# Inverting the delta rule's chunk matrices with one product and its transpose per level, in four quarters of the array

## The chip, the cores and the metric

The kernel runs on one NeuronCore of a Trainium2 chip. TensorE (PE in the profile) multiplies, VectorE (DVE), ScalarE (ACT) and GpSimd (POOL) do the elementwise work, SyncE (SP) issues the loads. The metric is device time in microseconds (us) of one launch; less is better. A difference is a change if it exceeds what repeated runs of one kernel differ by.

## The reference

A 512-token sequence of width 1024 goes through two blocks in float32: a hybrid mixer (gated delta rule with 4 heads of 128, beside a convolution of 31 taps), cross attention over a memory, a convolved feed-forward, then a retention layer and a stick-breaking attention layer. The part that matters here is the chunked delta rule, 8 chunks of 64 tokens for each of 4 heads:

```
kb = kc * bc[..., None]
L = jnp.where(strict, jnp.einsum('nbhid,nbhjd->nbhij', kb, kc) * decay, 0.0)
rhs = jnp.concatenate([vc * bc[..., None], kb * jnp.exp(gc)[..., None]], axis=-1)
sol = lax.linalg.triangular_solve(eye + L, rhs, left_side=True, lower=True, unit_diagonal=True)
```

So 32 unit lower triangular 64x64 matrices `I + L` have to be inverted (or solved with). The kernel forms the inverses on TensorE by doubling: blocks of 1, 2, 4, ..., 32 are joined until the 64x64 block is inverted.

## The kernel before

Large projections fill most of the program. A weight slab of 128x1024 is loaded, rounded to its high part by ACT (L1307) and its low part by DVE (L2054), and then multiplied with the activations in three matmuls of 512 columns for each of 8 steps of the contraction (L507 to L509): 24 large matmuls to a slab. Small work is laid between them by "beats": after the third, sixth and eighth step of a slab (so after 9, 9 and 6 large matmuls) each of three lanes of generator functions goes on to its next `yield`. All engines tick the same lanes in the same places, each in its own program order, and wait for each other by semaphores.

The delta rule is a lane function `chain(p)`, one for each pair of heads p = 0, 1; each handles 16 matrices (2 heads x 8 chunks). Even chunks lie on partitions 0 to 63 and odd ones on 64 to 127 (`RR`), so a 64x64 product has its operands and its result in one half: product after product alternates between the upper left and the lower right quarter of the array. `chain(0)` starts with the slab of the first GLU, `chain(1)` 27 beats later. The order in a chain is: Gram matrices (`kk`), transposes of v, `qk`, then the inverse, then keys, `u`, `w`, eight state steps of two beats each (`ws`, then `kv` and `o`), and a transpose of the output (`otr`): 37 ticks. From the first tick of `chain(1)` to the end of the keys-and-gates section there are 3 + 12 + 20 = 35 beats; whatever is left then runs without large matmuls between it (`fg.drain()`).

The inverse keeps the current block inverse both ways round: `UTT` (transposed) and `UT`. At each of the levels 2, 4, 8, 16, 32 POOL masks `UL` to the block that joins (`LM`, L3070), TensorE multiplies it with `UT` (`lt`, 16 products), DVE forms I minus that (`UX`, L2188), and at the next beat TensorE makes the new transposed inverse (`tt`, 16 products) and the new plain one (`tx`, 16 products, left out at the last level). DVE copies the one out of PSUM (L2198; at the last level in two halves into `UTF`, L2203), ACT the other (L1439). The first level, blocks of 1, is done elementwise on DVE (L2178, L2181), and its transpose `tl` is 16 products with the identity. So a level takes two beats. The products of pair 0 use tiles `km`, `u_xq` and `u_x`, those of pair 1 `u_t`, `u_rq` and `u_r`; all are issued by the helper `one` at L512. The results go to banks 4 and 5 (pair 0) or 2 and 3 (pair 1). DVE also works on the convolutions meanwhile: four taps for each conv tile (L2106 to L2114) and the 31 taps of two of the four long convolutions (L2266, L2271), the other two going through ACT (L1505) and POOL (L3090).

Of the kernel before, what the change touches and what calls it, by code (L numbers as in the profile page):

```python
# [1 line left out]

# [31 lines left out]
CSH = ["id64", "mc", "ms", "m1t", "m2t", "m4t", "m8t", "m16t", "m32t"]  # L34
# [132 lines left out]
def program(nc, A, out):  # L167
    root = ExitStack()
    with root:
# [11 lines left out]
        PS = [root.enter_context(nc.psum_tensor(f"ps{i}", [128, 512], F32)) for i in range(8)]  # L181
# [165 lines left out]
        LM = [[R3[p][:, i * 512:i * 512 + 512] for i in range(2)] for p in range(2)]  # L347
        KBANK = ((4, 5), (2, 3))
        WQ = [x[:].rearrange("p (g y c) -> p g y c", y=4, c=64) for x in (XWQ, UWQ)]
# [12 lines left out]
        LEVELS = (2, 4, 8, 16, 32)  # L362
# [130 lines left out]
        def tensor_program(e):  # L493
# [17 lines left out]
            def one(dst, a, b, start, stop):  # L511
                return e.matmul(dst, a, b, start=start, stop=stop, skip_group_check=True)  # L512
# [178 lines left out]
            def chain(p):  # L691
# [31 lines left out]
                pe.wait_ge(*gdv[(p, "tt", 0)])  # L723
                for h, tb, par in CHUNKS:
                    o = (h * 4 + tb) * 64
                    R = RR[par]
                    t = one(b[R, o:o + 64], UTT[p][R, o:o + 64], csh["id64"][R, :], True, True)
                t.then_inc(*gmm((p, "tl")))
                rel[A_] = [(gac, (p, "tl", 0))]
                yield  # L730
                for n_ in range(5):
                    b = bank(A_)
                    pe.wait_ge(*gac[(p, "tl", n_)])
                    pe.wait_ge(*ggp[(p, "lm", n_)])
                    for h, tb, par in CHUNKS:
                        o = (h * 4 + tb) * 64
                        R = RR[par]
                        t = one(b[R, o:o + 64], LM[p][n_ % 2][R, o:o + 64], UT[p][R, o:o + 64], True, True)
                    t.then_inc(*gmm((p, "lt", n_)))
                    rel[A_] = [(gdv, (p, "xx", n_))]  # L740
                    yield
                    b = bank(B_)
                    pe.wait_ge(*gdv[(p, "xx", n_)])
                    pe.wait_ge(*gdv[(p, "tt", n_)])
                    for h, tb, par in CHUNKS:
                        o = (h * 4 + tb) * 64
                        R = RR[par]
                        t = one(b[R, o:o + 64], UX[p][R, o:o + 64], UTT[p][R, o:o + 64], True, True)
                    t.then_inc(*gmm((p, "tt", n_)))
                    rel[B_] = [(gdv, (p, "tt", n_ + 1))]  # L750
                    if n_ < 4:
                        b = bank(A_)
                        for h, tb, par in CHUNKS:
                            o = (h * 4 + tb) * 64
                            R = RR[par]
                            t = one(b[R, o:o + 64], UTT[p][R, o:o + 64], UX[p][R, o:o + 64], True, True)
                        t.then_inc(*gmm((p, "tx", n_)))
                        rel[A_] = [(gac, (p, "tl", n_ + 1))]
                    yield
# [8 lines left out]
                for h in range(2):  # L768
                    b = bank(KBANK[p][h])
                    pe.wait_ge(*gdv[(p, "tt", 5)])  # L770
# [517 lines left out]
        def scalar_program(e):  # L1288
# [134 lines left out]
            def chain(p):  # L1423
# [8 lines left out]
                ac.wait_ge(*gmm[(p, "tl")])  # L1432
                e.activation(UT[p], PS[KBANK[p][0]][:], ACT.Copy).then_inc(*gac((p, "tl", 0)))
                yield
                for n_ in range(5):
                    yield
                    if n_ < 4:
                        ac.wait_ge(*gmm[(p, "tx", n_)])
                        e.activation(UT[p], PS[KBANK[p][0]][:], ACT.Copy).then_inc(*gac((p, "tl", n_ + 1)))  # L1439
                    yield  # L1440
# [596 lines left out]
        def vector_program(e):  # L2037
# [104 lines left out]
            def chain(p):  # L2142
# [23 lines left out]
                for h in range(2):  # L2166
# [11 lines left out]
                e.scalar_tensor_tensor(g3(UTT[p]), g3(UL[p]), -1.0, bm(csh["m1t"], 8), ALU.mult, ALU.mult).then_inc(  # L2178
                    *gdv((p, "tta")))
                ve.wait_ge(*gdv[(p, "tta")])  # L2180
                e.tensor_tensor(g3(UTT[p]), g3(UTT[p]), bm(csh["id64"], 8), ALU.add).then_inc(*gdv((p, "tt", 0)))  # L2181
# [4 lines left out]
                for n_ in range(5):  # L2186
                    ve.wait_ge(*gmm[(p, "lt", n_)])
                    e.scalar_tensor_tensor(g3(UX[p]), g3(A_[:]), -1.0, bm(csh["id64"], 8), ALU.mult, ALU.add).then_inc(  # L2188
                        *gdv((p, "xx", n_)))
# [5 lines left out]
                    yield  # L2195
                    ve.wait_ge(*gmm[(p, "tx" if n_ < 4 else "tt", n_)])
                    if n_ < 4:
                        e.tensor_copy(UTT[p], B_[:]).then_inc(*gdv((p, "tt", n_ + 1)))  # L2198
                    else:
                        ve.wait_ge(*zero["utf"])  # L2200
                        for par in range(2):
                            R = RR[par]
                            t = e.tensor_copy(UTF[R, :, R], g3(B_[:])[R])  # L2203
                        t.then_inc(*gdv((p, "tt", 5)))
                    yield
# [783 lines left out]
        def pool_program(e):  # L2989
# [64 lines left out]
            def chain(p):  # L3054
# [12 lines left out]
                yield  # L3067
                for n_, s in enumerate(LEVELS):
                    po.wait_ge(*(gmm[(p, "lt", n_ - 2)] if n_ >= 2 else gdv[(p, "lt")]))
                    e.tensor_tensor(g3(LM[p][n_ % 2]), g3(UL[p]), bm(csh[f"m{s}t"], 8), ALU.mult).then_inc(  # L3070
                        *ggp((p, "lm", n_)))
                    if n_ == 1:
                        yield
                    if n_ >= 1:
                        yield
                        yield
                for _ in range(2):
                    yield
# [167 lines left out]
def constants():  # L3246
# [7 lines left out]
    m = {"id64": p == c, "mc": p <= c, "ms": p < c, "m1t": (p // 2 == c // 2) & (p < c)}  # L3254
    for s in (2, 4, 8, 16, 32):
        m[f"m{s}t"] = (p // (2 * s) == c // (2 * s)) & ((c // s) % 2 == 1) & ((p // s) % 2 == 0)
# [83 lines left out]
```

## Time and profile before

| | us |
|---|---|
| median of 3 runs (lowest, highest) | 1689.42 (1689.4, 1689.75) |
| the profiled execution | 1689.16 |
| its span in the profile | 1687.2 |
| PE busy | 1665.5 |
| DVE busy | 1049.7 |
| ACT busy | 738.7 |
| POOL busy | 188.5 |

The profiled execution is the one whose rows are read below; what lies around its span is 1.96 us. A busy PE says that some matmul was in flight, so it is no proof that PE sets the time; the chain of waits says which engine did. The granted TensorE clock is 1.00 of full speed (2.4 GHz) throughout.

### The profile page before, as it was taken

What the parts mean: (1) busy time and instruction counts of PE and PEld (TensorE: products, weight loads), DVE (VectorE), ACT (ScalarE), POOL (GpSimd) and SP (SyncE); (2) the same over time, 40 slices, a digit from 0 to 9 for tenths busy, and PEclk for the clock granted to TensorE, in tenths of its full rate; (3) what the DMA queues carried; (4) which work ended last, traced back from release to release, by engine and by line L of the source; (5) the groups of instructions that cost most, each with busy time, mean ns of one, the idle gap of its engine ahead of it and who ended that gap; (6) DMA issues with size and microseconds to landing.
All of it is one profiled execution on the core that took longest, in us unless ns stands there. A gap on an engine that the chain in (4) does not pass through costs nothing.

```text
span 1687.2 us, 23136 instructions
## 1 busy us (share of the span) xinstructions
PE 1665.5 (99%) x9357; PEld 1403.4 (83%) x9357; DVE 1049.7 (62%) x1567; ACT 738.7 (44%) x1137; POOL 188.5 (11%) x170
## 2 busy tenths in 40 slices
PE   9999999999999999999999999999999999999998
PEld 7787897987898888888988888888898888888887
DVE  7889798474489349549675643655574545354445
ACT  6654477553553223223542323323364645253462
POOL 0455470300300000000100000000100000000001
PEclk9999999999999999999999999999999999999999
DMA  6112134421223323323322213213212222222221
GB/s 218 60 44 63 52 106 132 139 75 51 78 73 113 102 73 118 104 78 100 119 88 81 100 51 106 100 60 110 76 66 79 72 78 86 75 88 75 87 75 51
DMA packets 45576, 147.67 MB, mean 88 GB/s; under 512 B 5024, under 2 KB 8992, under 8 KB 45472
## 3 DMA queue, kind: packets, MB, share of 16 engines
q1 hardware_dynamic: 45472, 146.21, 26.3%
q8 instruction: 75, 1.23, 0.3%
q14 instruction: 29, 0.24, 0.0%
HBM read 144.09 MB, written 2.10 MB: 87 GB/s over the span
## 4 chain that ended last, share of the span: by engine, by line
PE 84%; DVE 11%; ACT 2%; issue 2%; POOL 0%; DVEq 0%; ACTq 0%; POOLq 0%
PE ps L507 21%; PE ps L509 21%; PE ps L508 21%; PE ps L512 20%; DVE sl L2054 2%; DVE ps L2271 1%; DVE ps L2114 1%; DVE y L2478 1%; DVE xl L2495 1%; DVE ps L2108 0%; ACT sh L1307 0%; DVE h L2488 0%; DVE pad L2106 0%; PE ps L1128 0%; DVE ss L2232 0%
## 5 line engine op out<-in xcount | busy, mean ns | idle before, releaser
L1307 ACT ACTIVATE sh<-raw 128x1024 fp32r<-128x1024 f32 x257 | 268.2, 1053 | 372.8 <-PE ps L509 256.7
L2054 DVE TENSOR_TENSOR sl<-raw,sh 128x1024 fp32r<-128x1024 f32 x257 | 321.7, 1259 | 131.5 <-ACT sh L1307 131.4
L507 PE MATMUL ps<-xh,sh 128*128 128x512 f32 (+1 forms) x664 | 262.9, 396 | 0.0
L509 PE MATMUL ps<-xl,sh 128*128 128x512 f32 (+1 forms) x664 | 253.9, 382 | 0.0
L508 PE MATMUL ps<-xh,sl 128*128 128x512 f32 (+1 forms) x664 | 253.8, 382 | 0.0
L507 PE MATMUL ps<-sh,xh 128*128 128x512 f32 x384 | 151.8, 395 | 0.0
L509 PE MATMUL ps<-sl,xh 128*128 128x512 f32 x384 | 149.7, 390 | 0.0
L508 PE MATMUL ps<-sh,xl 128*128 128x512 f32 x384 | 149.7, 390 | 0.0
L509 PEld LDWEIGHTS ps<-xl,sh 128*128 128x128 f32 x664 | 124.8, 188 | 24.9
L507 PEld LDWEIGHTS ps<-xh,sh 128*128 128x128 f32 x664 | 124.9, 188 | 24.5 <-issue 0.7
L508 PEld LDWEIGHTS ps<-xh,sl 128*128 128x128 f32 x664 | 125.1, 188 | 22.7 <-issue 0.7
L3013 POOL TENSOR_TENSOR dg<-dg,sq 128x512 f32<-128x512 f32 (+1 forms) x27 | 30.2, 1119 | 829.4 <-ACT sq L1313 828.1
L507 PE MATMUL ps<-x2hu,sh 128*128 128x256 f32 (+1 forms) x346 | 118.3, 342 | 0.0
L509 PE MATMUL ps<-x2lu,sh 128*128 128x256 f32 (+1 forms) x346 | 115.8, 335 | 0.0
L508 PE MATMUL ps<-x2hu,sl 128*128 128x256 f32 (+1 forms) x346 | 115.1, 333 | 0.0
L507 PE MATMUL ps<-x2hd,sh 128*128 128x512 f32 (+1 forms) x300 | 103.7, 346 | 0.1
L509 PE MATMUL ps<-x2ld,sh 128*128 128x512 f32 (+1 forms) x300 | 102.4, 341 | 0.0
L508 PE MATMUL ps<-x2hd,sl 128*128 128x512 f32 (+1 forms) x300 | 102.1, 340 | 0.0
L3090 POOL TENSOR_TENSOR acc<-acc,ca 128x512 f32<-128x512 f32 x60 | 85.3, 1422 | 66.6 <-ACT ca L1505 62.2
L509 PEld LDWEIGHTS ps<-sl,xh 128*128 128x128 f32 x384 | 72.1, 188 | 15.6
L508 PEld LDWEIGHTS ps<-sh,xl 128*128 128x128 f32 x384 | 72.2, 188 | 15.2 <-issue 0.5
L507 PEld LDWEIGHTS ps<-sh,xh 128*128 128x128 f32 x384 | 72.1, 188 | 15.2 <-issue 0.5
(438 smaller groups left out, 3320.4 us busy)
## 6 DMA issues: line engine op xcount, KB each, us to landing
raw<-in_wup SPq DMA_DIRECT2D x44, 512.0 KB, 3.5
raw<-in_wdn SPq DMA_DIRECT2D x24, 512.0 KB, 3.5
raw<-in_rqk SPq DMA_DIRECT2D x16, 512.0 KB, 3.6
raw<-in_rv SPq DMA_DIRECT2D x16, 512.0 KB, 3.4
raw<-in_rg SPq DMA_DIRECT2D x16, 512.0 KB, 4.3
raw<-in_rout SPq DMA_DIRECT2D x16, 512.0 KB, 3.5
raw<-in_sv SPq DMA_DIRECT2D x16, 512.0 KB, 3.4
raw<-in_sg SPq DMA_DIRECT2D x16, 512.0 KB, 3.5
```

The source lines that it names most:

```text
L507: e.matmul(dst, wh, ah, start=start, stop=False, skip_group_check=True)
L508: e.matmul(dst, wl, ah, start=False, stop=False, skip_group_check=True)
L509: return e.matmul(dst, wh, al, start=False, stop=stop, skip_group_check=True)
L512: return e.matmul(dst, a, b, start=start, stop=stop, skip_group_check=True)
L1307: e.activation(SH[j % NSPL][:], RAW[j % NRAW][:], ACT.Copy).then_inc(*hi(j))
L2054: e.tensor_tensor(SL[j % NSPL][:], RAW[j % NRAW][:], SH[j % NSPL][:].bitcast(F32), ALU.subtract).then_inc(*lo(j))
L2114: e.scalar_tensor_tensor(C[:], PAD[:, 1 + q:1 + q + T], prm("gconv", tile * 4 + q), C[:], ALU.mult, ALU.add).then_inc(*cv((n, "t", q) if q ...
L2271: e.scalar_tensor_tensor(tap_sum(c, q), src, w, tap_sum(c, q - 1), ALU.mult, ALU.add).then_inc(*tpd((c, q)))
L2478: e.scalar_tensor_tensor(Y[:, k, c], Y[:, k, c], prm(gpost[0], gpost[1] + k), PS[0][:, 0:256] if b == 5 and hf else YR[:, c], ALU.mult, AL ...
L2495: e.scalar_tensor_tensor(lo_[:, k, c], H[:, k, c], prm(g[0], g[1] + k), hi_[:, k, c].bitcast(F32), ALU.mult, ALU.subtract).then_inc(*s2((k ...
L3013: e.tensor_tensor(SA[:, c], SA[:, c], SQ[(k - 1) % 2][:] if k < 4 else half(SQ, k % 4), ALU.add).then_inc(*sa(("y", b, k)))
L3090: e.tensor_tensor(ACC[:, c, :], ACC[:, c, :], gpb[("tmp", c, q)], ALU.add).then_inc(*tpp((c, q)))
```

## The change

The recurrence is another one. With `d = 2I + L^T`, and `e_s` = half the identity minus the joining block of level s (masks made on the host), `z = d * e_s` elementwise, and the next `d` and its transpose are one product each: `UT^T Z` and `Z^T UT`. There are six levels (1, 2, 4, 8, 16, 32), each in one beat with two groups of 16 products that both wait for the same two things: ACT's copy of `d` and DVE's masked copy `z`. The last level has only one group, and DVE subtracts the identity as it writes `UTF`. The masks on POOL are gone, and so are DVE's `UX` and its plain copies. The chain has 33 ticks where it had 37.

The second head of the pair changes sides at each level: of its products, those that read partitions 0 to 63 write 64 to 127 at one level, and back at the next. In a row of four products (two heads, two chunks) each then has a quarter of the array of its own. The two heads' results go to two banks; the transposed products use banks 6 and 7, and all of PSUM is now one tensor, so that one instruction of ACT or DVE reads both banks.

```diff
-CSH = ["id64", "mc", "ms", "m1t", "m2t", "m4t", "m8t", "m16t", "m32t"]
+CSH = ["id64", "mc", "ms", "e1", "e2", "e4", "e8", "e16", "e32"]
...
+        UZ = [(UTT[p], UX[p]) for p in range(2)]
...
+        def heads(p, i):
+
+            b = 6 if i else KBANK[p][0]
+            return PSUM[:, b * 512:b * 512 + 1024].rearrange("p (h q b c) -> p h q b c", h=2, q=2, c=64)[:, :, 0]
...
-                pe.wait_ge(*gdv[(p, "tt", 0)])
+                pe.wait_ge(*gdv[(p, "d1t")])
...
-                for n_ in range(5):
-                    b = bank(A_)
-                    pe.wait_ge(*gac[(p, "tl", n_)])
-                    pe.wait_ge(*ggp[(p, "lm", n_)])
-                    for h, tb, par in CHUNKS:
...
-                        t = one(b[R, o:o + 64], LM[p][n_ % 2][R, o:o + 64], UT[p][R, o:o + 64], True, True)
...
-                    yield
...
-                        t = one(b[R, o:o + 64], UX[p][R, o:o + 64], UTT[p][R, o:o + 64], True, True)
...
-                            t = one(b[R, o:o + 64], UTT[p][R, o:o + 64], UX[p][R, o:o + 64], True, True)
...
+                for n_ in range(6):
+                    Z = UZ[p][n_ % 2]
+                    pe.wait_ge(*gac[(p, "d", n_)])
+                    pe.wait_ge(*gdv[(p, "z", n_)])
+                    for lhs, rhs, i in ((UT[p], Z, 1), (Z, UT[p], 0))[:2 if n_ < 5 else 1]:
+                        two = (6, 7) if i else KBANK[p]
+                        b2 = [bank(k) for k in two]
+                        for tb, h, par in product(range(NB), range(2), range(2)):
+                            o = (h * 4 + tb) * 64
+                            R, RO = (RR[(par + h * m) % 2] for m in (n_, n_ + 1))
+                            t = one(b2[h][RO, tb * 64:tb * 64 + 64], lhs[R, o:o + 64], rhs[R, o:o + 64], True, True)
...
-                for n_ in range(5):
-                    ve.wait_ge(*gmm[(p, "lt", n_)])
-                    e.scalar_tensor_tensor(g3(UX[p]), g3(A_[:]), -1.0, bm(csh["id64"], 8), ALU.mult, ALU.add).then_inc(
...
+                for n_ in range(6):
+                    ve.wait_ge(*gmm[(p, "dt", n_)])
+                    if n_ < 5:
+                        e.tensor_tensor(b4(UZ[p][(n_ + 1) % 2]), heads(p, 1), bm4(csh[f"e{LEVELS[n_ + 1]}"]),
+                                        ALU.mult).then_inc(*gdv((p, "z", n_ + 1)))
...
-                for n_, s in enumerate(LEVELS):
...
-                    e.tensor_tensor(g3(LM[p][n_ % 2]), g3(UL[p]), bm(csh[f"m{s}t"], 8), ALU.mult).then_inc(
...
+                for _ in range(10):
                     yield
```

How the rows stand on PE in the inverse of pair 0, one helper line for all products (L512 before, L525 after; `x16` is 16 products). Before, from the first `lt`:

```order
L512 MATMUL ps<-u_xq,u_x 64x64 x16
L507 MATMUL ps<-xh,sh 128x512
L508 MATMUL ps<-xh,sl 128x512
L509 MATMUL ps<-xl,sh 128x512
...
L512 MATMUL ps<-km,u_xq 64x64 x16
L512 MATMUL ps<-u_xq,km 64x64 x16
L507 MATMUL ps<-xh,sh 128x512
```

After, from the same place in the slab (`km` and `u_xq` are `z` and `d` here; at every second level both lie in `u_xq`, hence one row of x32):

```order
L525 MATMUL ps<-km,u_xq 64x64 x16
L525 MATMUL ps<-u_xq,km 64x64 x16
L520 MATMUL ps<-xh,sh 128x512
L521 MATMUL ps<-xh,sl 128x512
L522 MATMUL ps<-xl,sh 128x512
...
L525 MATMUL ps<-u_xq 64x64 x32
L520 MATMUL ps<-xh,sh 128x512
```

Two groups now stand at every beat, where one and two alternated. On DVE in the same place, before:

```order
L2188 SCALAR_TENSOR_TENSOR u_xq<-ps,ch 128x512
L2193 TENSOR_TENSOR qk<-qk,u_x 128x512
L2194 COPY eg<-u_x 128x8
L2241 SCALAR_TENSOR_TENSOR x2lu<-gt,prm,x2hu 128x256
L2198 COPY km<-ps 128x512
L2241 SCALAR_TENSOR_TENSOR x2lu<-gt,prm,x2hu 128x256
L2316 TENSOR_TENSOR vf<-ps,rb 128x512
L2054 TENSOR_TENSOR sl<-raw,sh 128x1024
L2188 SCALAR_TENSOR_TENSOR u_xq<-ps,ch 128x512
```

And after (L2188 is now the masked copy `z`, L2200 and L2201 the scaling of q by its decay and a small copy, L2053 the slab's low part):

```order
L2188 TENSOR_TENSOR u_xq<-ps,ch 128x512
L2200 TENSOR_TENSOR qk<-qk,u_x 128x512
L2201 COPY eg<-u_x 128x8
L2238 SCALAR_TENSOR_TENSOR x2lu<-gt,prm,x2hu 128x256
L2188 TENSOR_TENSOR km<-ps,ch 128x512
L2200 TENSOR_TENSOR qk<-qk,u_x 128x512
L2201 COPY eg<-u_x 128x8
L2238 SCALAR_TENSOR_TENSOR x2lu<-gt,prm,x2hu 128x256
L2313 TENSOR_TENSOR vf<-ps,rb 128x512
L2053 TENSOR_TENSOR sl<-raw,sh 128x1024
L2188 TENSOR_TENSOR u_xq<-ps,ch 128x512
```

The second scaling of q and its small copy have moved up: they now stand between the second `z` and the third, ahead of the slab's low part.

## Rows read from the trace of the kernel before

**Rows 1.** The page: busy time by engine, and the shares of the chain.
```profile
PE 1665.5 (99%) x9357; PEld 1403.4 (83%) x9357; DVE 1049.7 (62%) x1567; ACT 738.7 (44%) x1137; POOL 188.5 (11%) x170
PE 84%; DVE 11%; ACT 2%; issue 2%; POOL 0%; DVEq 0%; ACTq 0%; POOLq 0%
```
**Rows 2.** Chain, 99:165: start us, us, engine, written tile, line.
```profile
99.95 0.75 DVE ps L2271
...
159.49 1.66 DVE u_t L2181
161.28 1.15 PE ps L512 x32
```
**Rows 3.** Windows: stretch, its length, busy PE, PEld, DVE, ACT, POOL, clock, DMA.
```profile
84.00:100.00 16.00, 16.00 (x271) 13.08 (x268) 12.34 (x17) 8.07 (x17) 14.08 (x13) 1.00 0.17 57
100.00:115.00 15.00, 15.00 (x134) 12.51 (x133) 14.74 (x25) 8.07 (x11) 6.28 (x6) 1.00 0.12 38
145.00:160.00 15.00, 13.23 (x87) 11.00 (x87) 14.59 (x28) 8.04 (x12) 12.44 (x9) 1.00 0.23 71
220.00:240.00 20.00, 20.00 (x136) 18.04 (x135) 19.56 (x34) 12.78 (x20) 15.72 (x11) 1.00 0.33 106
```
**Rows 4.** Timeline, PE: start us, us, engine, line, operation, tiles, shapes, count [idle].
```profile
71.64 0.40 PE L508 MATMUL ps<-xh,sl 128*128 128x512 f32 x1
71.87 0.39 PE L509 MATMUL ps<-xl,sh 128*128 128x512 f32 x1
...
72.56 0.39 PE L509 MATMUL ps<-xl,sh 128*128 128x512 f32 x1
72.88 1.15 PE L512 MATMUL ps<-u_xq,u_x 64*64 64x64 f32 x32
...
74.30 0.40 PE L508 MATMUL ps<-xh,sl 128*128 128x512 f32 x1
...
75.25 0.39 PE L509 MATMUL ps<-xl,sh 128*128 128x512 f32 x1
75.56 1.15 PE L512 MATMUL ps<-km,u_xq 64*64 64x64 f32 x32
76.54 1.10 PE L512 MATMUL ps<-u_xq,km 64*64 64x64 f32 x32
...
77.91 0.40 PE L508 MATMUL ps<-xh,sl 128*128 128x512 f32 x1
```
**Rows 5.** Windows of 0.02 us at a group's start, its own instructions alone.
```profile
72.90:72.92 0.02, 0.02 (x2) 0.02 (x2) 0.00 (x0) 0.00 (x0) 0.00 (x0) 1.00 0.00 0
72.98:73.00 0.02, 0.02 (x4) 0.02 (x6) 0.00 (x0) 0.00 (x0) 0.00 (x0) 1.00 0.00 0
```
**Rows 6.** Timeline, PE: products of other shapes, and waits.
```profile
67.28 1.15 PE L512 MATMUL ps<-qk 128*64 128x64 f32 x32
69.51 1.15 PE L512 MATMUL ps<-ch,km 64*64 64x64 f32 x32 [1.08 <-DVE km L2181]
...
111.29 1.95 PE L512 MATMUL ps<-u_xq,km 128*128 128x128 f32 x16
...
161.28 1.15 PE L512 MATMUL ps<-ch,u_t 64*64 64x64 f32 x32 [0.49 <-DVE u_t L2181]
...
262.87 1.06 PE L820 MATMUL ps<-idn,qk 128*128 128x128 f32 x8 [1.44 <-ACT qk L1460]
```
**Rows 7.** Timeline, DVE.
```profile
67.00 0.69 DVE L2178 SCALAR_TENSOR_TENSOR km<-u_l,ch 128x512 f32<-128x512 f32 x1
...
74.08 0.69 DVE L2188 SCALAR_TENSOR_TENSOR u_xq<-ps,ch 128x512 f32<-128x512 f32 x1 [1.26 <-PE ps L512]
74.69 1.25 DVE L2193 TENSOR_TENSOR qk<-qk,u_x 128x512 f32<-128x512 f32 x1
...
79.72 2.32 DVE L2054 TENSOR_TENSOR sl<-raw,sh 128x1024 fp32r<-128x1024 f32 x1
```
**Rows 8.** Lines, POOL, 60:210: count, busy us, mean ns.
```profile
L3070 POOL TENSOR_TENSOR u_x<-u_l,ch 128x512 f32<-128x512 f32 x5 | 8.3, 1671 | 0.8 <-DVE u_l L2175 0.8
```

More of the change, by code:

```diff
@@ L1 @@
 from contextlib import ExitStack
+from itertools import product
 import numpy as np
@@ L179, in under @@
                 return alloc(ph, name, shape, dt)
-        PS = [root.enter_context(nc.psum_tensor(f"ps{i}", [128, 512], F32)) for i in range(8)]
+        PSUM = root.enter_context(nc.psum_tensor("ps", [128, 4096], F32))
+        PS = [PSUM[:, i * 512:i * 512 + 512] for i in range(8)]
         RAW = [alloc(root, f"raw{i}", [128, SLAB]) for i in range(NRAW)]
@@ L346, in program, with b4, bm4 @@
         UT, UX = ([R2[p][:, i * 512:i * 512 + 512] for p in range(2)] for i in range(2))
-        LM = [[R3[p][:, i * 512:i * 512 + 512] for i in range(2)] for p in range(2)]
+        UZ = [(UTT[p], UX[p]) for p in range(2)]
         KBANK = ((4, 5), (2, 3))
+        def heads(p, i):
+            b = 6 if i else KBANK[p][0]
+            return PSUM[:, b * 512:b * 512 + 1024].rearrange("p (h q b c) -> p h q b c", h=2, q=2, c=64)[:, :, 0]
+        def b4(x):
+            return x.rearrange("p (h b c) -> p h b c", h=2, c=64)
+        def bm4(x):
+            return x.unsqueeze(1).unsqueeze(1).broadcast_to([x.shape[0], 2, NB, x.shape[1]])
         WQ = [x[:].rearrange("p (g y c) -> p g y c", y=4, c=64) for x in (XWQ, UWQ)]
@@ L361, in program @@
         MSQK, RQK, NK, FJ, FK = 0, 2, 4, 5, 6
-        LEVELS = (2, 4, 8, 16, 32)
+        LEVELS = (1, 2, 4, 8, 16, 32)
         def sig(n, step=1):
@@ L1431, in chain @@
                     yield
-                ac.wait_ge(*gmm[(p, "tl")])
-                e.activation(UT[p], PS[KBANK[p][0]][:], ACT.Copy).then_inc(*gac((p, "tl", 0)))
-                yield
-                for n_ in range(5):
[L1436 to L1440, printed above, removed]
+                for n_ in range(6):
+                    ac.wait_ge(*gmm[(p, "d", n_)])
+                    dst, src = (b4(UT[p]), heads(p, 0)) if n_ else (UT[p], PS[KBANK[p][0]][:])
+                    e.activation(dst, src, ACT.Copy).then_inc(*gac((p, "d", n_)))
+                    yield
+                yield
                 yield
@@ L2185, in chain @@
                 yield
-                for n_ in range(5):
-                    ve.wait_ge(*gmm[(p, "lt", n_)])
-                    e.scalar_tensor_tensor(g3(UX[p]), g3(A_[:]), -1.0, bm(csh["id64"], 8), ALU.mult, ALU.add).then_inc(
-                        *gdv((p, "xx", n_)))
+                for n_ in range(6):
+                    ve.wait_ge(*gmm[(p, "dt", n_)])
+                    if n_ < 5:
+                        e.tensor_tensor(b4(UZ[p][(n_ + 1) % 2]), heads(p, 1), bm4(csh[f"e{LEVELS[n_ + 1]}"]),
+                                        ALU.mult).then_inc(*gdv((p, "z", n_ + 1)))
+                    else:
+                        ve.wait_ge(*zero["utf"])
+                        for par in range(2):
+                            R = RR[par]
+                            t = e.tensor_tensor(UTF[R, :, R].rearrange("p (h b) c -> p h b c", h=2), heads(p, 1)[R],
+                                                bm4(csh["id64"][R, :]), ALU.subtract)
+                        t.then_inc(*gdv((p, "tt")))
                     if n_ < 2:
@@ L3253, in constants @@
     p, c = p % 64, c[:, :64]
-    m = {"id64": p == c, "mc": p <= c, "ms": p < c, "m1t": (p // 2 == c // 2) & (p < c)}
-    for s in (2, 4, 8, 16, 32):
-        m[f"m{s}t"] = (p // (2 * s) == c // (2 * s)) & ((c // s) % 2 == 1) & ((p // s) % 2 == 0)
+    m = {"id64": p == c, "mc": p <= c, "ms": p < c}
+    for s in (1, 2, 4, 8, 16, 32):
+        block = (p // (2 * s) == c // (2 * s)) & ((c // s) % 2 == 1) & ((p // s) % 2 == 0)
+        m[f"e{s}"] = 0.5 * (p == c) - block
     csh = np.stack([m[n].astype(np.float32) for n in CSH], 1)
```

59 lines of the change are left out of this document (14 added, 45 removed).

## The prediction

> **What bounds the kernel now.** I read the page first: PE is busy for 1665.5 of 1687.2 us, and the chain that ended last is 84% PE and 11% DVE [rows 1]. A busy PE is no proof, so the chain of waits comes next, in the stretch that the change touches (about 67 to 265 us; nothing behind 265 is edited). From 70 to 99 us the chain lies on PE alone. From 99.95 us it is on DVE, convolution taps one behind the other, until DVE's L2181 ends at 161.15 and lets PE go on [rows 2]. The windows say the same: DVE is busy for 12.34 of 16 us between 84 and 100, but for 14.74 of 15 from 100 on, 14.59 of 15 before 160 and 19.56 of 20 between 220 and 240 [rows 3]. So PE time saved before 100 us and between 161 and 204 counts in full, and time saved elsewhere counts only as far as DVE can follow.
>
> **What a group of small products costs.** Between large matmuls PE starts one each 0.23 us (71.64 to 71.87). Around the single group at 72.88 two large ones start 1.74 us apart (72.56 to 74.30) with one between them, so the group costs 1.74 - 2 x 0.23 = 1.28 us. Around a pair of groups it is 75.25 to 77.91, 2.66 - 0.46 = 2.20 us [rows 4]. So a second group adds 0.92 us, and entering and leaving costs 1.28 - 0.92 = 0.36 us a visit.
>
> Where do the 0.92 us come from? A product shows as two records: 16 products are x32. At the start of a group, two are in flight at 72.90 and four at 72.98 [rows 5]: they start two at a time. A group with 128 rows and 64 columns takes the same 1.15 us as one with 64 by 64, and 16 records of the full array take 1.95 us [rows 6], which is (1.95 - 0.28) / 15 = 0.11 us each (0.28 us is one record's latency, estimated from the 0.22 us that the last 64-column record adds). Half of that is 0.056 us for a record of 64 columns, and 0.92 / 16 = 0.058 us is what a pair takes. So I read a group as two streams side by side, one in each half of the array, each at its own full rate. The products of the changed kernel alternate over four quarters; if four streams run, a group takes 0.92 / 2 = 0.46 us.
>
> **Part 1, fewer groups and fewer visits.** For each pair of heads the edited part has five single `lt` visits, four visits with `tt` and `tx`, and one with `tt` alone: 6 x 1.28 + 4 x 2.20 = 16.5 us. The first transpose is there in both. Now there are five visits of two groups and one of one. With four streams that is 5 x (0.36 + 0.92) + (0.36 + 0.46) = 7.2 us, 9.3 us less. With no more overlap than now it is 5 x 2.20 + 1.28 = 12.3 us, 4.2 us less. For both pairs: 18.6 us, or 8.4 us at the low end. I take 18.6: a row with two different streams of moving data on the same rows (the 128-row group) and one with two streams on different rows are both there, at one price, and the quarters only combine the two.
>
> The Trainium skill (TensorE: Matmul & The Clock Gate, Part 3) says that tiles of rows and columns compose and run side by side, which is this reading. The same page (Wait — 56ns, not 53.3ns?) says that matmuls never start less than about 25 ns apart however small they are; 32 records would then take 0.80 us and not 0.46, and by that rule the two pairs would save an estimated 11 us. The trace shows two starts within 0.02 us [rows 5], but a mean of 0.92 / 32 = 29 ns, so it does not exclude such a limit on the mean; it is part of the first rival.
>
> **Part 2, the start of the inverse.** PE waits 1.08 and 0.49 us for L2181 before the first transpose [rows 6]. That transpose now needs only the instruction before it; L2178 ends at 67.69 [rows 7], while PE is in the `qk` group until 68.43. Both waits go: -1.6 us. What is late next is `z` for the first level, one DVE instruction later, and PE has nine large matmuls (2.1 us) before it.
>
> **Part 3, four beats less.** `chain(1)` needs 37 ticks and gets 35 beats, so its last ticks run without cover, and PE waits 1.44 us for ACT before the last transpose [rows 6], about 0.5 us for a state step before it. With 33 ticks nothing is left over: -2.0 us. The gain has both bounds near: 1.4 if only the row shown goes, 2.4 with the pipeline's own ends.
>
> **Part 4, what DVE takes back.** Each level needed two beats and now has one, and the second scaling of q with its small copy come between the second and the third `z`. In the worst place for pair 0 DVE does, behind one `z`: 1.25 (scaling) + 0.69 (small copy) + 0.48 (the mem lane) + 0.69 + 1.2 to 2.3 (slab's low part) + 0.69 (the next `z`), 5.0 to 6.1 us; those without a row of their own are of the size of L2188, 0.69 us [rows 7]. PE has from one group's end to the group after the next 9 + 9 large matmuls and a visit, 4.1 + 1.3 = 5.4 us. So a wait of 0 to 1 us for each pair. The 2.32 us of L2054 [rows 7] came while POOL was masking, five times for about 1.67 us for a pair [rows 8]; those instructions are gone, so the short end is likelier. ACT's copy (one more for each pair) and the wait for banks 6 and 7 I cost at nothing: ACT has the same 1.4 us or more between groups as before, and both banks are free when `chain(0)` comes and two beats before `chain(1)` does.
>
> In the stretches that DVE ends, PE sheds more than the levels: keys, `u` and `w` move ahead, state steps move in. From 100 to 161 us DVE loses one L2188, two half copies and four key products, 7 x 0.69 = 4.8 us, and gets one more state step (under 1.4 us): -3.4 us. PE loses two groups (2.6 us) and the keys, and gets a step and the output's transpose. The two remain neck and neck, and where one leads for a slab the other's spare time is lost. Bounds: nothing lost, if DVE runs well ahead without POOL beside it; or everything that PE saves there, 2.6 us in the first stretch and about as much again as two visits and `u` with `w` (4 us) in the second. With the level waits that makes 0 to 8.6 us; I take +3.5, under the middle, since DVE's own work also falls.
>
> **Sum.** -18.6 - 1.6 - 2.0 + 3.5 = -18.7 us. From the profiled execution's own 1689.16 us that is 1670.5; the median of the runs shown is 0.26 us above that execution, so 1670.7, and I say 1671.
>
> **Rivals.**
> 1. *Two at a time is all there is* (a limit of issue, or of one half's columns, not of geometry). For: the 128-row and the 64-row group cost the same to a hundredth, which one limit on the stream of instructions would give too. Against: the full-array records at twice the price for twice the columns. Then 8.4 us are saved in part 1, DVE is followed more easily (+1.5): 1689.4 - 8.4 - 1.6 - 2.0 + 1.5 = 1679. With a limit between, 1674 to 1677. Chance 0.20.
> 2. *DVE takes it back.* Four streams run, but DVE ends the stretches from 100 to 161 and from 204 on as now, and the waits in the levels come out at their long end: +8.6 in place of +3.5, 1676; together with the first rival 1684. For: 14.74 of 15 us [rows 3]. Against: five fewer copies and no POOL beside it. Chance 0.12.
> 3. *The quarters get in each other's way* (slower). Two products that share a half's rows or a half's columns could exclude each other; then the 16 products go one at a time, two records of 0.058 us each: 1.87 us for a group. The eleven groups and six visits cost 11 x 1.87 + 6 x 0.36 = 22.7 us for a pair against 16.5 now, 12.4 us more for both, less 3.6 from parts 2 and 3, plus DVE's waits: 1699. It decides from a group of about (16.5 - 2.2) / 11 = 1.3 us on. Against: the 128-row group shows two products on the same rows together; nothing shows two on the same columns. Chance 0.04.
> The rest, 0.64, is the forecast.
>
> **How the numbers follow.** The likeliest case alone reaches from 1667 (nothing taken back) to 1675. The first two rivals lie at 1674 to 1684. With 1665 to 1682 I leave out a little of the second rival and the third. A measurement of this kernel can tell 0.2%, 3.4 us, from no change. Only rival 3, or rival 1 with all of rival 2 and some stall that I have not seen, comes to 1686 or above: faster 0.94, same 0.02, slower 0.04.
>
> **What would show it.** A single group of 16 records pairs within about 0.7 us (start to next large matmul) where 1.08 us stand now: four streams; 1.08 us again: rival 1; 2 us: rival 3. Six records in flight at 0.02 us from a group's start, where two are now, would show the quarters directly. The wait on the first transpose should be gone, and so should the 1.44 us before the last. In the chain of waits DVE should still hold the stretch of the convolutions; if its share of busy time there falls well below 0.9 while PE waits for it, part 4 is wrong in kind. A time above 1682 or new waits of over 1 us at several levels would make the prediction wrong.

## The result and the profile after

| | median us (lowest, highest) | ratio to before, 95% interval |
|---|---|---|
| before, measured beside it | 1689.56 (1689.4, 1689.75) | |
| after | 1669.4 (1668.88, 1671.05) | 0.9882 [0.9865, 0.9899] |

The change saves 20.2 us (forecast 18.7); the predicted 1671 is 1.6 us too high. The profiled execution took 1669.49 us, its span in the profile is 1667.4. The page of the kernel after, to set beside [rows 1]: busy time by engine, and the shares of the chain of waits.

```profile
PE 1647.4 (99%) x9165; PEld 1385.7 (83%) x9165; DVE 1041.4 (62%) x1559; ACT 740.5 (44%) x1139; POOL 171.6 (10%) x160
PE 83%; DVE 12%; ACT 2%; issue 2%; DMA 0%; SPq 0%; DVEq 0%; ACTq 0%
```

Its windows, with the columns of [rows 3]:

```profile
84.00:100.00 16.00, 14.74 (x168) 11.94 (x167) 13.68 (x20) 9.65 (x19) 10.28 (x9) 1.00 0.11 35
100.00:115.00 15.00, 13.70 (x75) 11.10 (x73) 13.77 (x21) 8.86 (x15) 5.92 (x5) 1.00 0.10 36
145.00:160.00 15.00, 12.66 (x148) 9.92 (x150) 13.52 (x22) 7.90 (x14) 8.57 (x7) 1.00 0.16 42
220.00:240.00 20.00, 19.65 (x123) 16.53 (x122) 19.66 (x28) 15.02 (x25) 16.07 (x11) 1.00 0.33 106
```

PE busy falls by 18.1 us (1665.5 to 1647.4) of the span's 19.8, so nearly all of the gain is work shed and little, on balance, is waits. DVE is still busy for 0.9 of the convolutions' stretch or more (13.77 of 15 us, 13.52 of 15, 19.66 of 20), and most of the chain of waits from 100 to 160 us still lies on it.

PE's timeline of the kernel after, to set beside [rows 4] (start us, us):

```profile
72.18 0.39 PE L522 MATMUL ps<-xl,sh 128*128 128x512 f32 x1
72.50 0.69 PE L525 MATMUL ps<-km,u_xq 64*64 64x64 f32 x32
73.02 0.65 PE L525 MATMUL ps<-u_xq,km 64*64 64x64 f32 x32
...
74.86 0.40 PE L522 MATMUL ps<-xl,sh 128*128 128x512 f32 x1
75.19 1.16 PE L525 MATMUL ps<-u_xq 64*64 64x64 f32 x64
76.28 0.50 PE L520 MATMUL ps<-xh,sh 128*128 128x512 f32 x1
76.61 0.40 PE L521 MATMUL ps<-xh,sl 128*128 128x512 f32 x1
```

From 74.86 to 76.61 are 1.75 us between large matmuls with one between (the row of x64 is two groups), so a visit of two groups costs 1.75 - 0.46 = 1.29 us, where it cost 2.20 before. The second group starts 0.52 us behind the first, where it was 0.98.

Windows of 0.02 us at the first group's start, its own instructions alone, for the kernel after, to set beside [rows 5]:

```profile
72.52:72.54 0.02, 0.02 (x4) 0.02 (x4) 0.00 (x0) 0.00 (x0) 0.00 (x0) 1.00 0.00 0
72.60:72.62 0.02, 0.02 (x6) 0.02 (x10) 0.00 (x0) 0.00 (x0) 0.00 (x0) 1.00 0.00 0
```

Four are in flight 0.02 us after the start, where two were. PE's other changed places and its waits, which answer to [rows 6]; first the timeline, then the larger waits from 60 to 265 us (releaser: us in total, times, longest), of the kernel after and then of the kernel before:

```profile
69.15 1.15 PE L525 MATMUL ps<-ch,u_l 64*64 64x64 f32 x32
94.40 2.35 PE L525 MATMUL ps<-u_xq,km 128*128 128x128 f32 x16 [1.23 <-DVE u_x L2210]
151.21 1.06 PE L822 MATMUL ps<-idn,qk 128*128 128x128 f32 x8 [2.00 <-ACT qk L1459]
155.80 1.15 PE L525 MATMUL ps<-ch,u_l 64*64 64x64 f32 x32
```
```profile
PE ps L822 <- ACT qk L1459: 2.0, 1, 2.0
PE ps L525 <- DVE ss L2229: 1.5, 2, 1.4
PE ps L525 <- DVE u_x L2210: 1.2, 1, 1.2
```
```profile
PE ps L512 <- DVE ss L2232: 2.1, 2, 1.7
PE ps L512 <- ACT u_xq L1453: 1.3, 1, 1.3
PE ps L512 <- DVE u_r L2213: 0.8, 1, 0.8
```

Both waits on the first transpose are gone, and so is the 1.44 us before pair 1's last one. New are 1.23 us before `u` of pair 0, and pair 0's own output transposes, which now wait 2.00 us. But the kernel before had other waits that are gone too: 1.28 us for ACT's first copy of `w` (L1453) at pair 0's first state step, 0.84 us before `u` of pair 1 (L2213), and 1.70 us for DVE (L2232) between the same two large matmuls as the 2.00 us now.

**How runs of one kernel differ.** Three things come and go between executions of these kernels, each worth about 1 us. In five of the fourteen profiles PE stands without a releaser in the middle of the fifth visit of pair 0's inverse ("issue", 0.4 to 0.7 us, and 0.7 to 1.0 from one large matmul to the next). In six of the ten that have a wait of about 2 us near 151 us, the granted clock falls behind it (0.9 to 1.6 us). And the first large matmul of the slabs starts anywhere from 28.06 to 28.95 us, at 28.12 in the profile before and 28.90 in the one after. The kernel after shows neither of the first two in its profile. So I give medians, and beside them, where 2 us matter, the lowest times or the shift between two profiles of one and the same large matmul, counted from the start of the program.

By that count the edited stretch gained a little more than the span says. The large matmul in front of pair 0's `qk` starts at 66.95 us before and 67.75 after, and one behind the last edited place at 284.58 and 264.73: 217.63 against 196.98 us, 20.6 us less. From there to the last large matmul both take 1392.0 us.

### The profile page after: what moved, and what is told of

Its sections match the earlier page's. It is cut to its first block, busy times and chain, and to the rows that moved or that the text cites. A ratio compares the mean times of both kernels' runs of the same rounds, so it can differ in the third digit from the quotient of the medians.

```text
span 1667.4 us, 22732 instructions
## 1 busy us (share of the span) xinstructions
PE 1647.4 (99%) x9165; PEld 1385.7 (83%) x9165; DVE 1041.4 (62%) x1559; ACT 740.5 (44%) x1139; POOL 171.6 (10%) x160
## 4 chain that ended last, share of the span: by engine, by line
PE 83%; DVE 12%; ACT 2%; issue 2%; DMA 0%; SPq 0%; DVEq 0%; ACTq 0%
PE ps L520 21%; PE ps L522 21%; PE ps L521 21%; PE ps L525 19%; DVE sl L2053 2%; DVE ps L2268 1%; DVE ps L2113 1%; DVE y L2475 1%; DVE xl L2492 1%; DVE ps L2107 0%; DVE h L2485 0%; PE ps L1130 0%; DVE pad L2105 0%; DVE ss L2229 0%; ACT sh L1309 0%
## 5 line engine op out<-in xcount | busy, mean ns | idle before, releaser
L2053 DVE TENSOR_TENSOR sl<-raw,sh 128x1024 fp32r<-128x1024 f32 x257 | 322.5, 1262 | 131.0 <-ACT sh L1309 130.9
```

The lines of the kernel that those rows point to most:

```text
L2053: e.tensor_tensor(SL[j % NSPL][:], RAW[j % NRAW][:], SH[j % NSPL][:].bitcast(F32), ALU.subtract).then_inc(*lo(j))
```

## The experiments

**Are the quarters what a group gains by?** Four kernels alter only which quarters the products of a group use, or their order.

```diff
 e1_no_side_change
-R, RO = (RR[(par + h * m) % 2] for m in (n_, n_ + 1))
+R, RO = RR[par], RR[par]
 e2_head_outermost
-for tb, h, par in product(range(NB), range(2), range(2)):
+for h, tb, par in product(range(2), range(NB), range(2)):
 e3_same_columns
+for c_, tb, h in product(range(2), range(NB), range(2)):
+    par = (c_ + h * (n_ + 1)) % 2
 e4_same_rows
+for r_, tb, h in product(range(2), range(NB), range(2)):
+    par = (r_ + h * n_) % 2
```

> The new recurrence, but the second head stays on its side at every level, so its products use the same two quarters as the first head's. Theory (two streams give way to four): a visit of two groups should cost 2.20 us again where the changed kernel has 1.29 (74.86 to 76.61, less two cadences of 0.23), ten visits of two and two of one, so 22 groups x 0.46 = 10.1 us more work on PE; because DVE ends part of the stretch, 6 to 10 us of it show: 1676 to 1680. Rival A (the groups run faster for another reason, such as results in two banks): the visit stays near 1.3 us and the time at 1669 to 1670. Rival B (DVE would have hidden nearly all of it): groups at 0.92 us but the time under 1673.

> The changed kernel with the same products in the same quarters, but issued head by head: eight products that alternate between two quarters, then eight that alternate between the two others. Theory 1 (products start in the order of the program, so only neighbours in that order can share the array): a group costs 0.92 us as without the side change, 1676 to 1680. Theory 2 (PE looks far enough ahead to start products of the other two quarters): groups stay near 0.5 us and the time at 1669 to 1670.

> The same products, issued so that eight in a row alternate between two quarters with the same columns and different rows (results to two banks), then eight of the other columns. Tells whether two products that share columns run side by side, which nothing before showed. If they do: 0.92 us a group, 1676 to 1680. If they exclude each other: 32 records of 0.058 us, 1.87 us a group, 22 groups x 1.4 = 31 us over the changed kernel, near 1700. If PE starts products far ahead: 0.5 us, 1670.

> The same products, issued so that eight in a row alternate between two quarters with the same rows and different columns, then eight of the other rows. The products of 128 rows and 64 columns already run two at a time, so 0.92 us a group, 1676 to 1680. If sharing rows of different data costs something, more than 0.92 us; if PE starts products far ahead, 0.5 us and 1670.

| | median us (lowest) | ratio to before | one visit of two groups, us |
|---|---|---|---|
| after | 1669.4 (1668.88) | 0.9882 [0.9865, 0.9899] | 1.29 |
| e1, two quarters | 1679.28 (1678.11) | 0.9934 [0.9917, 0.995] | 2.2 |
| e2, one head's pair of quarters after the other's | 1673.09 (1672.42) | 0.9901 [0.9886, 0.9915] | 1.7 |
| e3, pairs in the same columns | 1674.49 (1674.38) | 0.9907 [0.9888, 0.9927] | 1.7 |
| e4, pairs in the same rows | 1673.37 (1672.81) | 0.9901 [0.9881, 0.9921] | 1.7 |

The edits of e2 to e4 replace the same loop line of the changed kernel; e3 and e4 were run twice, the other experiments four or five times. e1's timeline of PE, and e3's, both in the place of the first level:

```profile
71.93 0.40 PE L522 MATMUL ps<-xl,sh 128*128 128x512 f32 x1
72.26 1.15 PE L525 MATMUL ps<-km,u_xq 64*64 64x64 f32 x32
73.24 1.10 PE L525 MATMUL ps<-u_xq,km 64*64 64x64 f32 x32
74.27 0.50 PE L520 MATMUL ps<-xh,sh 128*128 128x512 f32 x1
```
```profile
72.48 0.80 PE L525 MATMUL ps<-km,u_xq 64*64 64x64 f32 x26
73.07 0.27 PE L525 MATMUL ps<-u_xq,km 64*64 64x64 f32 x2
73.11 0.28 PE L525 MATMUL ps<-km,u_xq 64*64 64x64 f32 x3
...
73.24 0.80 PE L525 MATMUL ps<-u_xq,km 64*64 64x64 f32 x27
73.97 0.50 PE L520 MATMUL ps<-xh,sh 128*128 128x512 f32 x1
```

The side change alone is worth 9.9 us in medians: 0.92 us at each of ten visits and 0.45 at two, 10.1 in the two profiles. A group without it costs what it did before, though its results still go to two banks. So the overlap comes from the quarters, not from the banks or the new recurrence. The other half of the 20.2 us, some 10.3 between the kernel before and e1, is what fewer groups and visits and the other edits bring.

e2, e3 and e4 missed all their forecasts: neither no loss (a group of 0.46 us) nor a loss of all the overlap (0.92). All three lose 0.40 us at a visit of two groups and 0.28 at one of one, 4.6 us in the profiles (3.7, 5.1 and 4.0 in medians; the clock fell behind pair 0's wait in e3's and e4's profiles and not in e2's), whether the neighbours in the order share rows, columns or neither. In e3 the second group's records start among the last of the first group's. So PE starts products out of the next pair of quarters while an earlier pair still has some to start, but not so far ahead that it undoes runs of eight; how far was not measured. Whether two products lie above each other or side by side makes no difference that these runs show; that a product for each of the four quarters comes within any four in a row does.

**What took the first waits away?** e5 makes PE wait for one instruction more. e7 puts five masks of 128x512 back on POOL for each pair, in step with the levels; what they compute is not used (ACT's copy of `u` waits for the last of them).

```diff
 e5_first_transpose_late
-pe.wait_ge(*gdv[(p, "d1t")])
+pe.wait_ge(*gdv[(p, "z", 0)])
 e7_pool_masks_back
-for _ in range(10):
-    yield
+for n_ in range(5):
+    po.wait_ge(*(gmm[(p, "dt", n_ - 2)] if n_ >= 2 else gdv[(p, "d1t")]))
...
+    e.tensor_tensor(g3(R3[p][:, n_ % 2 * 512:n_ % 2 * 512 + 512]), g3(UL[p]), bm(csh["e1"], 8),
+                    ALU.mult).then_inc(*ggp((p, "lm", n_)))
...
```

> The changed kernel, but PE waits for the first masked copy z (the instruction behind d) before the first transpose of each pair, as it waited for L2181 before the change. Theory (part 2 of the prediction): the two waits come back, near 1.1 us for pair 0 and 0.5 us for pair 1, and both count: 1671.0. Rival: pair 0's wait is repaid, because PE waits again a few beats later for the keys' scaled copies (1.23 us in the changed kernel), which lie on DVE and do not move with PE: then only pair 1's 0.5 us shows, 1669.4 to 1669.9.

> The changed kernel with five mask multiplications of 128x512 for each pair put back on POOL beside the levels; their results are not used. The forecast held that POOL beside DVE stretches DVE's instructions (2.32 us for a slab's low part where it is 1.22 alone). Theory: DVE loses 4 to 6 us of speed, of which 1 to 3 us show: 1670.5 to 1672.5. Rival: DVE has slack in the levels, so nothing shows: under 1670.

e5: 1670.81 us (1669.81 to 1671.24), 0.9885 [0.987, 0.99]. Its median is 1.4 us above after's, but set beside after's profile the large matmuls move by only 0.2 us at pair 0's wait and by nothing at pair 1's. The rest of what this profile loses is the "issue" stall (0.8 us) and a fall of the clock (1.2 us), which come and go. The median lies at the 1671.0 of the theory, but not by its mechanism: the two waits do not come back. The rival's, 0.5 us at pair 1, is not there either. DVE in the kernel before and POOL beside it, then DVE and PE in e5:

```profile
67.72 1.64 DVE L2181 TENSOR_TENSOR km<-km,ch 128x512 f32<-128x512 f32 x1
```
```profile
67.04 3.45 POOL L3070 TENSOR_TENSOR u_x<-u_l,ch 128x512 f32<-128x512 f32 x2 [0.80 <-DVE u_l L2175]
```
```profile
68.12 0.69 DVE L2180 TENSOR_TENSOR km<-u_l,ch 128x512 f32<-128x512 f32 x1
```
```profile
67.68 1.15 PE L525 MATMUL ps<-qk 128*64 128x64 f32 x32
68.96 1.15 PE L525 MATMUL ps<-ch,u_l 64*64 64x64 f32 x32
```

The same form of DVE instruction took 1.64 us with POOL masking beside it and 0.69 without. That is 0.95 of the 1.08 us that PE waited; having one instruction fewer to wait for is worth the other 0.2.

e7: 1674.26 us (1673.43 to 1676.98), 0.9912 [0.9897, 0.9928], 4.9 above after, where 1 to 3 was expected. DVE's slab product stretches to 2.21 us, the `z` behind it ends late, and PE waits in the middle of pair 1's inverse. First DVE, then PE:

```profile
169.89 2.21 DVE L2054 TENSOR_TENSOR sl<-raw,sh 128x1024 fp32r<-128x1024 f32 x1
172.03 0.68 DVE L2189 TENSOR_TENSOR u_rq<-ps,ch 128x512 f32<-128x512 f32 x1
```
```profile
172.86 1.60 PE L525 MATMUL ps<-u_rq 64*64 64x64 f32 x64 [2.17 <-DVE u_rq L2189]
174.38 0.79 PE L520 MATMUL ps<-xh,sh 128*128 128x512 f32 x1
```

This is the wait that part 4 of the prediction feared, with POOL's masks there to cause it. In the profile it costs 2.7 us, and the large matmuls behind it, at a lower clock for a while, another 1.0; pair 0's first level loses 0.4. e7 does not bring the first wait back: its first mask starts at 67.63 us, 0.05 behind DVE's product of 67.58, which takes 0.69 us, where before POOL's stood first (67.04) and DVE's took 1.64. So the masks' part in that wait rests on the comparison above and on DVE's slab products, 2.2 us beside a mask in e7 and 1.22 alone, and not on a run that restores it. The profile also has the stall near 86 us (1.0 us) and the fall of the clock near 151 (1.6 us), so the 4.9 us of the medians may hold part of these.

**What are four beats worth?** e6 gives pair 1 its four beats back, as empty ones in the lanes of all engines (the edit shows PE's).

```diff
 e6_two_beats_pair_1
                     yield
+                    if p and n_ < 4:
+                        yield
```

> The changed kernel, but the first four levels of pair 1 take two beats each, so that its chain has 37 ticks again and outlives the 35 beats by two. The forecast's part 3 says 2.0 us for that (1.4 to 2.4). Where the keys-and-gates section ends the two traces should part by that; if DVE sets the time there, spreading the levels could also give back up to 2 us elsewhere. Expected: 1671.4. Rival (the run-out was not what cost, since the large alignment gain at that place comes from DVE's taps): within 0.5 us of the changed kernel.

1673.41 us (1671.47 to 1674.05), 0.9901 [0.9884, 0.9919]: +4.0 in medians, +2.6 between the lowest; expected were 2.0. The end of e6's drained ticks, PE, and the window around it:

```profile
243.50 0.71 PE L525 MATMUL ps<-vnz,u_a 128*128 128x128 f32 x4 [0.52 <-DVE vnz L2227]
245.65 1.78 PE L824 MATMUL ps<-idn,qk 128*128 128x128 f32 x8 [1.43 <-ACT qk L1463]
```
```profile
245.00:250.00 5.00, 4.35 (x16) 3.83 (x17) 1.36 (x4) 2.85 (x8) 0.00 (x0) 0.66 0.32 105
```

The waits come back as they were (0.52 and 1.43 us; 0.52 and 1.44 in the kernel before). Two things had not been counted. One is the time of the small products with nothing beside them, which stands as busy: in the kernel before, at the full clock, the drained products cost 4.29 us between two large matmuls, and the same products cost 1.93 between large matmuls in the kernel after, so the run-out is worth 2.4 us where its waits are 1.96. The other is the clock, 0.66 over 5 us in e6's profile: the large matmuls behind the run-out lose another 1.1 us. The fastest run of e6 had a mean clock of 1.000 over its whole span, the profiled one 0.998. A wait is dearer than its length.

**Is it the convolutions on DVE that take part of the gain back?** e8 is the kernel before and e9 the kernel after, both with 58 of DVE's 31-tap instructions cut to 64 of 512 columns, so most of the long convolution's sum is left out there.

```diff
 e8_before_short_taps, e9_after_short_taps
-e.scalar_tensor_tensor(tap_sum(c, q), src, w, tap_sum(c, q - 1), ALU.mult, ALU.add).then_inc(
+n_c = T if q in (TAP_HOP, 30) else 64
+e.scalar_tensor_tensor(tap_sum(c, q)[:, 0:n_c], src[:, 0:n_c], w, tap_sum(c, q - 1)[:, 0:n_c],
+                       ALU.mult, ALU.add).then_inc(
...
 e10_qscale_on_pool (the scalings of q and the small copies go from DVE to POOL)
+e.tensor_tensor(QK[:, h, :], QK[:, h, :], hd(R4[p], h), ALU.mult).then_inc(*ggp((p, "qe", h)))
+e.tensor_copy(EG[p][:, h, :], hd(R4[p], h)[:, 63:T:64]).then_inc(*ggp((p, "eg", h)))
```

> The kernel before, with 58 of DVE's long-convolution taps on 64 of 512 columns (for the channel tiles 1 and 3 most of the sum is left out), so that DVE no longer ends the stretches from 100 us on. Theory (DVE ends them): DVE's work falls by about 58 x 0.6 = 35 us and the waits of PE between 100 and 260 us, some 7 us, mostly go: 1680 to 1684. Rival (PE sets the time even there): under 2 us faster than before.

> The changed kernel with the same 58 taps shortened. Theory: with DVE out of the way the change is worth its full price, 18.6 + 1.6 + 2.0 = 22.2 us against the kernel before with short taps, so 1658 to 1662. Rival (DVE took nothing back; the 19.7 us measured are all there is): 19.5 to 20 us between the two.

> The changed kernel, but the two scalings of q and their small copies (L2200, L2201) are POOL's instead of DVE's. Theory (DVE's queue in the inverse still costs something): DVE sheds 2.5 us a pair there and the wait for the scaled keys shrinks: 1667 to 1668.5. Rival (POOL beside DVE is dearer than the work that it takes over, as the five masks were): the 128x512 products on POOL take some 1.7 us each and stretch DVE's, and the time stays or grows: 1669.5 to 1671.5.

e8: 1682.76 us (1682.54 to 1683.16), 0.996 [0.9945, 0.9975]. e9: 1663.38 us (1662.7 to 1664.07), 0.9845 [0.983, 0.9861]. e8 came as forecast: DVE's taps cost the kernel before 7 us. e9's theory, 22.2 us between the two, missed. Each gains 6 to 7 us by the shorter taps, and the change is worth 19.4 us between them, no more than the 20.2 with full taps. So these taps cost both kernels about the same and take back nothing of this change. That does not clear DVE as a whole: e9's profile still waits 1.18 us before `u`. e10: 1668.79 us (1668.65 to 1671.14), 0.9878 [0.9862, 0.9895]; 0.6 less than after in medians and 0.2 between the lowest, no difference that can be told. The wait before `u` is unchanged at 1.24 us. DVE in the kernel after shows why:

```profile
88.63 1.55 DVE L2053 TENSOR_TENSOR sl<-raw,sh 128x1024 fp32r<-128x1024 f32 x1
90.10 1.38 DVE L2194 TENSOR_TENSOR km<-ps,ch 64x512 f32<-64x512 f32 x2
91.51 0.79 DVE L2238 SCALAR_TENSOR_TENSOR x2lu<-gt,prm,x2hu 128x256 fp32r<-128x256 f32 x1
92.22 0.80 DVE L2263 TENSOR_SCALAR ps<-cp,prm 128x512 f32<-128x512 f32 x1
93.06 0.69 DVE L2209 TENSOR_TENSOR u_xq<-ps,smv 128x512 f32<-128x512 f32 x1
93.66 0.68 DVE L2210 TENSOR_TENSOR u_x<-ps,smp 128x512 f32<-128x512 f32 x1
```

`u` has one beat between the last level, whose products end at 88.63 us, and its start. In it DVE must write `UTF` (L2194) and scale the keys (L2209, L2210); a slab's low part (L2053) stands before that and two instructions of other lanes between. The scalings of q were done by 78 us.

**Can a beat cover the new waits?** Pair 0 has beats to spare, so e11 gives it one before `u`, and e12 one before its output transposes.

```diff
 e11_beat_before_u (PE; the same in DVE's, ACT's and POOL's lanes)
                     rel[KBANK[p][h]] = [(gdv, (p, "keys", h))]
                 yield
+                if not p:
+                    yield
 e12_beat_before_otr (PE; the same in ACT's lane)
                     yield
+                if not p:
+                    yield
                 for h in range(2):
                     b = bank(6 + h)
```

> The changed kernel, with one beat more for pair 0 between the transposes of the keys and u, in the lanes of PE, DVE, ACT and POOL alike. Theory: the ledger puts most of what pair 0 gives back at u, where PE waits 1.23 us for the scaled keys and its first product then comes 0.4 us later with nothing in flight; the beat of 9 large matmuls between covers that, and nothing is added, since pair 0 has beats to spare: 1667.5 to 1668. Rival: the four beats that pair 0 gains put all of its state steps earlier, and a beat more only moves the waits for DVE to another place (ss, vnz): 1669 to 1670.

> The changed kernel, with one beat more for pair 0 before the transposes of its output (PE's and ACT's lanes alone), so that they stand nine large matmuls later, ahead of pair 1's qk group. Nothing else moves. Theory (what the earlier beats gave back is a wait for ACT that a beat covers): the 2.0 us wait for ACT's last copy goes, with about 0.3 us of exposed start, and the transposes cost the same in the other beat: 1667.1. Rival (DVE ends this stretch whatever PE does, its taps in the chain of waits from 100 to 160 us): PE arrives earlier and waits as long for DVE's next results (v's transposes, z of pair 1): 1669 to 1669.8. Second rival: banks 6 and 7 come free a beat later, since ACT copies the transposes out behind its table load and a wait for DVE, and pair 1's first level waits: 1671 or above.

e11: 1674.84 us (1672.67 to 1675.3), 0.9907 [0.9893, 0.9922], 5.4 slower than after, against both expectations. The wait of 1.23 us before `u` goes, as the theory had it. But ACT's copy of `w` now comes behind another lane's L1401, which waits for DVE. ACT in e11, then PE:

```profile
101.81 0.60 ACT L1401 ACTIVATE qk<-ps 128x512 f32<-128x512 f32 x1 [2.68 <-DVE ps L2117]
102.31 0.59 ACT L1453 ACTIVATE u_xq<-ps 128x512 f32<-128x512 f32 x1
```
```profile
104.56 0.91 PE L525 MATMUL ps<-ss,u_xq 128*128 128x128 f32 x4 [2.26 <-ACT u_xq L1456]
...
157.24 1.94 PE L824 MATMUL ps<-idn,qk 128*128 128x128 f32 x8 [3.76 <-ACT qk L1463]
```

From 115 to 150 us e11 is within 1.4 us of after, mostly ahead, if both are counted from 67 us. Then it loses 7.3 us in one visit: the beat moves ACT's last copy of pair 0 behind a table load (1.28 us) and a wait of 2.43 us for DVE in the same queue (L1539), PE waits 3.76 us, and the granted clock is 0.61 from 155 to 160 us.

e12: 1670.43 us (1669.16 to 1672.19), 0.9885 [0.9868, 0.9901], 1.0 above after in medians, 0.3 between the lowest. The theory (1667.1) is wrong and the first rival's mechanism is right: the 2.00 us wait for ACT is gone and one of 2.11 us for DVE stands in its place (v's transposes need a bank that L2172 frees). Its range, 1669 to 1669.8, holds the lowest time and not the median. What this profile shows besides is the clock behind the wait; PE's timeline, and the window:

```profile
151.72 0.92 PE L724 MATMUL ps<-idn,u_rq 128*128 128x128 f32 x4 [2.11 <-DVE u_rq L2172]
...
152.87 0.63 PE L521 MATMUL ps<-xh,sl 128*128 128x512 f32 x1
153.30 0.63 PE L522 MATMUL ps<-xl,sh 128*128 128x512 f32 x1
```
```profile
150.00:155.00 5.00, 3.28 (x10) 2.71 (x11) 4.62 (x6) 4.20 (x6) 4.71 (x3) 0.70 0.29 105
```

Large matmuls start 0.43 us apart, where they start 0.23 apart at the full clock. No version was found that beats the changed kernel by more than can be measured.

## Why the prediction was right, point by point

The forecast's own case held, inside its range. Measured against its terms, by the profiles' 20.6 us for the edited stretch:

- **The cost of a group and part 1 (-18.6).** Right in mechanism and size. A visit of two groups was worked out at 1.28 us and is 1.29. Summed over the timeline by the prediction's own rule (the time over two gaps between large matmuls, less two regular ones), pair 0's ten visits cost 16.5 us before and its six cost 7.3 after: 9.2 us less, where 9.3 stood, and pair 1's the same: 18.5. The reading from [rows 4 to 6], two streams each at its own rate, did it; e1 shows that the quarters carry 9.9 us of it. The Trainium skill (TensorE: Matmul & The Clock Gate, Part 3) says that small tiles of the array run side by side, and these traces agree: 1.29 us a visit with four quarters and 2.2 with two. Its floor of about 25 ns between starts (Wait — 56ns, not 53.3ns?) does not hold here: 32 records start in 0.52 us, 16 ns each, and the 0.80 us a group that it would give is ruled out. A small thing was wrong: six records were forecast in flight after 0.02 us, and there are four, twice the two of before.
- **Part 2 (-1.6).** The amount was right (1.15 us at pair 0 and 0.6 at pair 1 between the two profiles, where 1.08 and 0.49 stood), the reason was not, and that is luck. The step "that transpose now needs only the instruction before it" is worth 0.2 us at pair 0 by e5 and nothing at pair 1. L2181 took 1.64 us while POOL masked beside it, and those masks went with the same change. The prediction had that stretching in [rows 8] and used it for part 4, but not for its own part 2.
- **Part 3 (-2.0).** Right in mechanism, 0.4 us too small: 2.4 us in the profiles of the kernels before and after, at the bound of 2.4. The waits that it summed are there; the uncovered products come on top. Where the clock falls behind the run-out it costs more, 4.0 us in e6's medians.
- **Part 4 (+3.5).** This is the term that was furthest off. 18.5 + 1.7 + 2.4 = 22.6 us were saved and 20.6 are left, so 2.0 came back and not 3.5. The number was picked from the range of 0 to 8.6, and the places are mostly not those it named. Inside the levels only 0.4 us is lost, at the first level of pair 1, and e8 against e9 shows that the 31 taps take nothing. From 90 to 118 us, at `u` and the first state steps of pair 0, PE gives back 3.0 us: `u` waits for DVE's scaled keys and starts exposed (its visit takes 3.73 us, large matmul to large matmul, and took 1.93 before), and the visit at 105 us waits for DVE twice (0.34 and 0.28 us) where the kernel before did not, and a state step at 115 us waits 1.35 us; this is net of the 1.28 us wait for ACT that is gone. Another 0.6 us goes at 264 us, where a later product now waits for DVE. Against that, 1.1 us is won at `u` of pair 1, whose 0.84 us wait is gone; why, no run tells. The other places together win 0.9 us, net. The 2.00 us before pair 0's output transposes is no net loss. It is a wait for ACT, whose copy stands behind one that waits 3.68 us for the short convolution's L2113 on DVE, but before, PE waited 1.70 us between the same two large matmuls and 0.34 us for the transposes later.
- **Rivals.** The first (two at a time) is excluded by the visit of 1.29 us, for which it had 2.20. The second (DVE takes back all) fell: 2.0 us came back and not 8.6. e7 shows what held it off: with POOL's masks left in place the kernel is 4.9 us slower in medians, near that rival's time. The third (quarters exclude each other) is excluded by e3 and e4, where sharing columns or rows for whole runs of products still leaves a group faster than before.

The forecast of 1671 was 1.6 us too high, mostly because part 4 was taken 1.5 us too large, and part 3 0.4 too small. That part 2 came out right owes to an effect that its step does not name.

## What to carry to other kernels

In these runs small fp32 products of 64x64 ran four at a time when any four neighbours in the order lay in four different quarters of the array (1.29 us for two groups, 2.2 with two quarters only); with runs of eight in two quarters, 0.40 of the 0.92 us was lost again. Before a DVE instruction's time is used in a sum, look at what POOL does beside it: an edit that takes POOL work away can shorten DVE's instructions in other places too (1.64 to 0.69 us here). A spare beat is not free even when nothing is added: it moves a lane's instructions on all engines to behind other lanes', and a copy on ACT that stands behind a waiting one can cost more than the wait that the beat covered.

## What the runs showed of the hardware that was not expected

- PE starts some of its small products out of their order, but not so far ahead that runs of eight in two quarters cost nothing: a pair of groups takes 1.29 us with four quarters in each four products, 1.7 with two quarters for eight products at a time, and 2.2 with two quarters only.
- A wait of PE of about 2 us may or may not be followed by the lower clock. Behind 1.98 to 2.00 us the granted clock stayed at 1.00 in the profiles of after, e2, e6 and e10; behind 1.97 to 2.11 us in those of e1, e3, e4, e5, e7 and e12 it fell, to 0.76 and 0.70 over 5 us in e5 and e12. Each time three to seven large matmuls start 0.43 instead of 0.23 us apart, and with those at the edges that costs 0.9 to 1.6 us.
- Five products of 128x512 on POOL, for each pair, beside DVE, cost this kernel 4.9 us in medians, although nothing computes with their results; 4.0 us of it can be placed in e7's profile.
